# Gathering the rows of 64 of 512 prompt tokens in an expert-retrieval kernel, and multiplying the other 448 densely

## The reference, cut to what matters

```python
qry = (x @ w_query).reshape(tokens, 8, 2, 128)
s = einsum('thjd,jkd->thjk', qry, keys)
s_top, i_top = top_k(s, 16)
cand = s_top[:, :, 0, :, None] + s_top[:, :, 1, None, :]
cand_idx = i_top[:, :, 0, :, None] * 128 + i_top[:, :, 1, None, :]
best, pos = top_k(cand.reshape(tokens, 8, 256), 16)
idx = take_along_axis(cand_idx.reshape(tokens, 8, 256), pos)
gates = softmax(best)
act = gelu(einsum('thkd,td->thk', peer_u[idx], x))
out = einsum('thk,thkd->td', gates * act, peer_v[idx])
```

## Time and profile before

| | |
|---|---|
| median of three runs | 2342.01 us |
| the profiled execution, its own time | 2342.8 us |
| its span in the trace | 2341.0 us |
| mean granted clock of TensorE, share of full speed | 0.973 |
| busy share: TensorE, VectorE, ScalarE, GpSimd | 95%, 64%, 36%, 47% |
| DMA: bytes moved, mean rate | 392.79 MB, 168 GB/s |
| hide stage, units 0 to 127 | 852.8 to 1625.8 us |
| value products | 1625.8 to 2325 us |

### The profile page before, as it was taken

The page is one execution under the profiler, slowest core; times in us unless marked ns, Lnnn a source line. Parts: engine busy times, 40 slices in busy tenths (PEclk is TensorE's granted clock), DMA queues, the critical chain, the costliest instruction groups (busy, mean ns, idle before and its releaser), DMA issues.

```text
span 2341.0 us, 32763 instructions
## 1 busy us (share of the span) xinstructions
PE 2216.4 (95%) x12345; PEld 1887.8 (81%) x12345; DVE 1509.6 (64%) x3040; ACT 841.9 (36%) x1146; POOL 1099.7 (47%) x620
## 2 busy tenths in 40 slices
PE   5999999986998899999999999999999999999997
PEld 3998899864766888888887888888888888888886
DVE  4676569565554678887898786664655555555551
ACT  3433445563124233333243444453422222222221
POOL 1332336226443410877877656842644444444441
PEclk8999999996998999999999999999999999999998
DMA  8122122475656755777767897876754554554530
GB/s 281 56 91 72 44 75 90 123 198 175 187 185 233 258 164 144 153 143 146 144 132 157 222 273 197 177 186 202 276 202 181 213 191 170 215 197 169 207 144 36
DMA packets 320590, 392.79 MB, mean 168 GB/s; under 512 B 52305, under 2 KB 262629, under 8 KB 320194
## 3 DMA queue, kind: packets, MB, share of 16 engines
q1 hardware_dynamic: 216770, 302.86, 41.6%
q10 hardware_dynamic: 58768, 58.76, 7.5%
q0 software_dynamic: 44928, 29.51, 7.0%
HBM read 305.70 MB, written 81.39 MB: 165 GB/s over the span
## 4 chain that ended last, share of the span: by engine, by line
PE 45%; POOL 12%; issue 3%; DMA 2%; DVE 1%; ACT 0%; DVEq 0%; ACTq 0%; POOLq 0%
PE bank L2740 30%; PE bank L2169 13%; POOL gates_scattered_dram L2357 12%; PE bank L2686 2%; DMA gates_scattered_dram<-sel 2%; DMA work<-sample_rows_dram 1%; DVE harea L2159 0%; DVE work L2582 0%; PE bank L2692 0%; DVE harea L2145 0%; POOL work L2338 0%; PE bank L2760 0%; DVE work L2089 0%; DVE work L2105 0%; DVE work L2414 0%
## 5 line engine op out<-in xcount | busy, mean ns | idle before, releaser
L2169 PE MATMUL bank<-pH,harea 128*128 128x512 f32 x2048 | 647.7, 393 | 1.3 <-DVE harea L2159 1.3
L2357 POOL DMA_INDIRECT gates_scattered_dram<-sel x256 | 433.9, 1695 | 222.4 <-DVE sel L2420 94.6
L2169 PEld LDWEIGHTS bank<-pH,harea 128*128 128x128 f32 x2048 | 386.0, 188 | 82.2 <-DVE harea L2159 1.7
L2169 PE MATMUL bank<-pL,harea 128*128 128x512 f32 x1024 | 399.6, 390 | 0.0
L2740 PE MATMUL bank<-area,work 128*128 128x512 f32 x1536 | 350.8, 389 | 0.0
L2740 PEld LDWEIGHTS bank<-area,work 128*128 128x128 f32 x1536 | 288.4, 188 | 59.8
L2740 PE MATMUL bank<-harea,pH 128*128 128x512 f32 x1024 | 315.9, 390 | 0.0
L2346 POOL TENSOR_TENSOR work<-work,work 128x1024 fp32r<-128x1024 f32 x64 | 155.6, 2433 | 216.7 <-ACT work L2607 216.7
L2159 DVE TENSOR_TENSOR harea<-harea,harea 128x1024 fp32r<-128x1024 f32 x128 | 156.7, 1224 | 144.5 <-PE bank L2169 143.0
L2346 POOL TENSOR_TENSOR pL<-work,pH 128x1024 fp32r<-128x1024 f32 x64 | 155.2, 2426 | 194.0 <-ACT pH L2607 194.0
L824 POOL TENSOR_TENSOR wL_in<-wb_in,wH_in 128x1024 fp32r<-128x1024 f32 x52 | 129.4, 2489 | 240.7 <-ACT wH_in L777 240.7
(11 more groups left out here) (546 smaller groups left out, 3547.5 us busy)
## 6 DMA issues: line engine op xcount, KB each, us to landing
harea<-in_peer_u_dram SPq DMA_DIRECT2D x256, 256.0 KB, 10.0
work<-in_peer_v_dram SPq DMA_DIRECT2D x64, 1024.0 KB, 4.9
hidden_dram<-harea ACTq DMA_DIRECT2D x64, 512.0 KB, 2.7
wb_in<-in_w_in_dram SPq DMA_DIRECT2D x26, 1024.0 KB, 5.1
wstage<-in_w_ada_dram SPq DMA_DIRECT2D x32, 512.0 KB, 5.1
gates_scattered_dram<-work POOLq DMA_DIRECT2D x32, 512.0 KB, 5.6
gates_dram<-area ACTq DMA_DIRECT2D x8, 2048.0 KB, 12.5
area<-hidden_dram SPq DMA_DIRECT2D x16, 1024.0 KB
```

Source lines behind the costliest of these rows:

```text
L2169: mm = self.nc.tensor.matmul(self.pa[u % 2][:, :], w[:, k, :], x[:, k, :], start=(n == 0), stop=(n == 3 * KD - 1))
L2357: pool.indirect_dma_start(out=cells, out_offset=bass.IndirectOffsetOnAxis(ap=address_of[i][:, n:n + 1], axis=0), in_=gate_of[i][:, n:n + 1 ...
```

## The change

The constants become TG = 64, TD = 448, SC = 1. The last 64 prompt tokens, 448 to 511, no longer take part in the dense computation; they are treated as the sample tokens are.

- *Dense part.* hide and products have 448 columns, not 512; hidden activations, gates, weights and their buffers shrink alike.
- *Selection order.* TILES = (3, 0, 1, 2): tile 3, which holds the gathered tokens, is selected first, then tile 0, the only one that is scattered. The tokens 384 to 447 and the tiles 1 and 2 are placed in quads: 80 in all, 16 of them in every second unit from 26 to 56, the other 64 in units 74 to 121. Scatters are 128 and are spread over units 31 to 107 (scatters_by_unit), no longer ahead of the loop.
- *Buffers.* There is one staging buffer, so that each block's first eviction waits for the store of the block before it, and two PSUM banks for quads, not four. The freed memory holds the gathered rows: two of peer_u, four of peer_v.
- *Gathered tokens.* One token a unit, from unit 40: TensorE broadcasts token n's x to all partitions with two 512-column matmuls into two PSUM banks (cast, at the end of unit 40 + n, when dot n-1 is done); GpSimd gathers its 128 rows of peer_u (512 KB) up to two tokens ahead; VectorE takes the 128 dots at the end of loop 41 + n, reading x from PSUM. Every fourth unit ScalarE takes the Gelu of four tokens' dots, VectorE weighs them, GpSimd gathers four tokens' rows of peer_v (2 MB), and TensorE adds them up in eight float32 matmuls into a third bank (mix_gathered, 16 times, units 50 to 110). At the end the sums are turned and added to x.
- *Query phase.* 16 float32 matmuls turn the 64 tokens' x at n = 4; ScalarE rounds them into pH and pL at n = 6, VectorE subtracts at n = 7; SyncE's first load of peer_u waits for this turn and not for the sample tokens'.
- *Sample tokens.* Their mixes go to one PSUM bank in place of two, with the same number of matmuls.

The diff, cut to its core:

```diff
-SC = 2
+SC = 1
+TG = 64
+TD = T - TG
+TILES = (3, 0, 1, 2)
+SCATTERED = 1
...
-    for u in range(58, 74, 2):
+    for u in range(26, 58, 2):
         counts[u] = 1
-    total = (NC - SC) * L // 4
+    total = (TD - SC * L) // 4
...
+def scatters_by_unit():
+    counts = [0] * UNITS
+    for u in range(31, 40):
+        counts[u] = 2
+    for u in range(40, 80):
+        counts[u] = 2 if u % 4 != 3 else 0
+    for u in range(90, 107):
+        counts[u] = (1 if u < 99 else 2) if u % 4 != 3 else 0
+    counts[107] = SC * P - sum(counts)
...
+    STORED = [12, 13] + list(range(4, 12))
+    DOTS, GELUS, WEIGHS, GATHERS, MIXES = 40, 45, 48, 47, 50
...
-        stage = [carve(sc, 4096 * i, (P, NG, JG, TB)) for i in range(2)]
+        stage = carve(sc, 0, (P, NG, JG, TB))
+        vg = [carve(sc, 4096 + D * i, (P, D)) for i in range(4)]
+        ug = [carve(work, 9616 + D * i, (P, D)) for i in range(2)]
...
+            def gather_hidden(n):
...
+                if n >= 2:
+                    pool.wait_ge(G["dotted"], n - 1)
+                pool.indirect_dma_start(out=ug[n % 2], out_offset=None, in_=A["peer_u"][0], in_offset=index(n)).then_inc(G[f"ug_in{n % 2}"], 16)
+            def gather_values(i):
+                if i:
+                    pool.wait_ge(G["mixed"], i)
+                for n in range(4):
+                    pool.indirect_dma_start(out=vg[n], out_offset=None, in_=A["peer_v"][0], in_offset=index(4 * i + n)).then_inc(G["vg_in"], 16)
...
+                n = u - DOTS - 1
+                if 0 <= n < TG:
+                    dve.wait_ge(G[f"ug_in{n % 2}"], 16 * (n // 2 + 1))
+                    dve.wait_ge(G["cast"], n + 1)
+                    V.tensor_tensor_reduce(out=halves(ug[n % 2]), in0=halves(ug[n % 2]), in1=banks[:, 2:4, :], scale=1.0, scalar=0.0,
+                                           op0=ALU.mult, op1=ALU.add, accum_out=dot_g[:, n:n + 1]).then_inc(G["dotted"], 1)
...
-                b, blk = q // PER_BLOCK % 2, q // PER_BLOCK
-                if q % PER_BLOCK == 0 and blk >= 2:
-                    act.wait_ge(m[f"stored{b}"], 16 * (blk // 2))
+                blk, n = divmod(q, PER_BLOCK)
+                if n == 0 and blk:
+                    act.wait_ge(m["stored0"], 16 * blk)
...
+            def cast(n):
...
+                    pe.wait_ge(G["dotted"], n)
+                for half, x in enumerate((S.pH, S.pL)):
+                    mm = nc.tensor.matmul(bank[2 + half].rearrange("p (k n) -> p k n", k=KD), pick_g[:, n:n + 1].to_broadcast((P, P)), x[:, :, TD:T], start=True, stop=True)
+                mm.then_inc(G["cast"], 1)
+            def mix_gathered(n):
+                pe.wait_ge(G["weighed"], n + 1)
+                pe.wait_ge(G["vg_in"], 64 * (n + 1))
...
+                if DOTS <= u < DOTS + TG:
+                    cast(u - DOTS)
+                if u >= MIXES and (u - MIXES) % 4 == 0 and (u - MIXES) // 4 < TG // 4:
+                    mix_gathered((u - MIXES) // 4)
...
-                    mm = nc.tensor.matmul(bank[k], v[s][:, j, cols], w[s][:, j, :], start=(start and x == 0), stop=(stop and x == 2))
+                    mm = nc.tensor.matmul(bank[k][:, 0:TD], v[s][:, j, cols], w[s][:, j, :], start=(start and x == 0), stop=(stop and x == 2))
```

More of the change, by code:

```diff
@@ L1870, in _ @@
                     A_(halves(rows[:, :]), pt[0:B, :, :], ACT.Copy).then_inc(q["s_row"], 1)
+                if n == 6:
+                    act.wait_ge(q["x_turned"], 1)
+                    for half, x in enumerate((PH_, PL_)):
+                        rounded = A_(x[:, :, TD:T], pt[:, half, :].rearrange("p (k n) -> p k n", k=KD), ACT.Copy)
+                    rounded.then_inc(q["x_rounded"], 1)
             for n in range(CHUNKS - 2, CHUNKS):
@@ L1928, in _ @@
                     mm.then_inc(q["s_turned"], 1)
+                if n == 4:
+                    pe.wait_ge(q["s_row"], 1)
+                    for k in range(KD):
+                        for at in (0, TG):
+                            mm = nc.tensor.matmul(pt[at:at + TG, k // 4, k % 4 * P:k % 4 * P + P], hT[:, k, TD:T], S.ident[:, :], start=True, stop=True)
+                    mm.then_inc(q["x_turned"], 1)
                 if n >= 2:
@@ L2123, in __init__ @@
         self.u, self.ut, self.uv = S.hu, S.ut, S.uv
-        self.ge = [carve(S.harea, 6144 + 1024 * i, (P, 2, T)) for i in range(2)]
+        self.ge = [carve(S.harea, 6144 + 1024 * i, (P, 2, TD)) for i in range(2)]
         self.utH = carve(S.harea, 8192, (P, 3, KD, P), F32R)
@@ L2206, in quads_by_unit @@
     return [range(first[u], first[u + 1]) for u in range(UNITS)]
+def scatters_by_unit():
[7 more added lines that the diff above has]
+    counts[107] = SC * P - sum(counts)
+    first = [sum(counts[:u]) for u in range(UNITS + 1)]
+    assert first[UNITS] == SC * P and counts[107] > 0
+    return [range(first[u], first[u + 1]) for u in range(UNITS)]
 def expert_phase(nc, A, S, O, gates, scattered, hidden_dram, sample_rows):
@@ L2436, in select @@
                 elif s == 5:
-                    if i < SC:
+                    if i == SCATTERED:
                         dve.wait_ge(m["gates"], i + 1)
-                        K.gates(own, gate_of[i])
+                        K.gates(own, gate_of[0])
                     K.numbers(own, 0)
@@ L2520, in samples, with gathered @@
                     V.tensor_tensor(x_s, x_s, bcast(S.vec[:, V_GF:V_GF + KD], 2, B), ALU.mult).then_inc(e["s_y"], 1)
+            def gathered(u):
+                if u == 24:
+                    dve.wait_ge(m["res_s"], 1)
+                    V.tensor_tensor(pick_g[:, :], S.ident[:, 0:TG], S.ident[:, TG:P], ALU.add)
+                    V.memset(w_g[:, :, :, :], 0.0).then_inc(G["picked"], 1)
+                    own(V.tensor_scalar(act_g[:, :], S.sel[:, 0, TD:T], float(NKEY), None, ALU.mult))
+                    own(V.tensor_tensor(act_g[:, :], act_g[:, :], S.sel[:, 1, TD:T], ALU.add))
+                    V.tensor_copy(eu_g[:, :], act_g[:, :]).then_inc(G["numbered"], 1)
+                n = u - DOTS - 1
[4 more added lines that the diff above has]
+                                           op0=ALU.mult, op1=ALU.add, accum_out=dot_g[:, n:n + 1]).then_inc(G["dotted"], 1)
+                i = (u - WEIGHS) // 4
+                if (u - WEIGHS) % 4 == 0 and 0 <= i < TG // 4:
+                    dve.wait_ge(G["gelued"], i + 1)
+                    if i:
+                        dve.wait_ge(G["mixed"], i)
+                    pair = lambda t: t.rearrange("p (a b) -> p a b", a=2)
+                    V.tensor_tensor(w_g[:, :, :, 31], pair(act_g[:, 4 * i:4 * i + 4]), pair(S.sel[:, 2, TD + 4 * i:TD + 4 * i + 4]), ALU.mult).then_inc(G["weighed"], 1)
+                if u == MIXES + TG - 4 + 3:
+                    dve.wait_ge(G["turned"], 1)
+                    for k in range(KD):
+                        x = S.xT[:, k, TD:T].rearrange("p (i r) -> p i r", r=2)
+                        at = k % 4 * P + TG * (k // 4)
+                        last = V.scalar_tensor_tensor(out=x, in0=bank[5][:, at:at + TG].rearrange("p (r i) -> p i r", r=2), scalar=S.mod[:, 40 + k, 0:1],
+                                                      in1=x, op0=ALU.mult, op1=ALU.add)
+                    own(last)
             def weigh(s, j):
@@ L2541, in _ @@
                                        op0=ALU.mult, op1=ALU.add, accum_out=token[:, 0:1]))
-            own(V.tensor_scalar(token[:, 1:2], token[:, 0:1], float(P // TB * TB * JG), None, ALU.add))
             H.move_low(dve, 0)
@@ L2557, in _ @@
                 select_samples(u)
+                gathered(u)
                 samples(u)
@@ L2641, in _ @@
                     act.wait_ge(m["mixed_s"], B)
-                    nc.scalar.activation(halves(rows[0]), banks[:, 4:6, :], ACT.Copy).then_inc(m["mixed_rows"], 1)
+                    nc.scalar.activation(rows[0][:, 0:512], bank[4], ACT.Copy).then_inc(m["mixed_rows"], 1)
+                i = (u - GELUS) // 4
+                if (u - GELUS) % 4 == 0 and 0 <= i < TG // 4:
+                    act.wait_ge(G["dotted"], 4 * i + 4)
+                    nc.scalar.activation(act_g[:, 4 * i:4 * i + 4], dot_g[:, 4 * i:4 * i + 4], ACT.Gelu).then_inc(G["gelued"], 1)
+                if u == MIXES + TG - 4 + 1:
+                    act.wait_ge(G["mixed"], TG // 4)
+                    nc.scalar.activation(vg[0][:, 0:512], bank[5], ACT.Copy).then_inc(G["rows"], 1)
                 if u == 110:
@@ L2749, in group @@
                     for k in range(KD):
-                        if first and j == 0 and k == 4:
+                        if first and j == 0 and k == 2:
                             pe.wait_ge(e["s_row"], 1)
```

155 lines of the change are left out of this document (95 added, 60 removed).

## The result

The changed kernel takes 2390.74 us in the median of four runs (2389.05 to 2396.8), the kernel before 2342.68: a ratio of 1.0206 (95% interval 1.0186 to 1.0225). The forecast was 2349 us, with a range up to 2388. The profiled execution took 2396.8 us; its span is 2394.6, 53.6 longer than before's 2341.0. It is the slowest of the four, so that its rows show some 6 us more than the loss of 48 between the medians.

The account below looks back on a forecast made before the run. TensorE was taken to bound both expert stages. The terms -83 - 13 + 35 + 66 - 9 + 3 + 8 = +7 on the profiled 2342.8 us gave about 2349 us, with an 8-in-10 range of 2288 to 2388.

Parts of the forecast that it names:

- The clock, +8: TensorE, after store stalls and heavy loops: five gaps each lose 1.7 us to the 1.2 GHz level; +8 us (0 to 20).
- Products and the hide stage's matmuls, -83 each: Both expert stages on TensorE: 3072 matmuls each 27.1 ns shorter, -83 us a stage; new TensorE work nearly cancels the hide stage's.
- The lateness of the stores, +45: Units 74 to 103: gate-store landings beyond 12.5 us stall TensorE through the single staging buffer; 45 us of that stretch's +66.
- 9.1 / (1 - 0.488) = 17.8, so I go by that quotient: Stores of gates: shortest landing divided by the engines' share left beside GpSimd's queue, matching a landing of 17.6 us beside gathers.
- the share of 0.66: Units 80 to 91: GpSimd's queue share with sample gathers on top, giving 27 us landings and 14 us stall at two block ends.
- Units 41 to 73, +35: VectorE becomes the bound and casts wait for dots: 228 us against 193.2, +35 us (bounds +17 to +45).
- Units 104 to 127, -9: Last hide units: each 0.65 us shorter, less three more quads and two more mixes; -9 us.
- The query phase, +3: Query phase: 16 added fp32 matmuls on TensorE at 0.22 us each, nothing waiting for them; +3 us (0 to 5).
- Stores in time: Faster rival: gate-store landings stay under 12.5 us, so the 45 and the clock's 8 go; 2296 us, chance 0.26.
- Everything hidden: Faster rival: VectorE's overrun is absorbed too; 2252 us, chance 0.06.
- Late gathers: Slower rival: gathered rows arrive late, each of 64 tokens losing 0.6 us, 38 us more; 2387 us, chance 0.17.
- The pace that doesn't follow the columns: Slower rival: the weight load, not the column count, sets the matmul pace; 166 us more, 2515 us, chance 0.03.

Follow-up runs that it names:

- the run with many widths: Kernel before, with value products of 512 down to 256 columns across the eight output blocks: products in 602.6 us, 202.5 ns a matmul at 448 columns.
- the long runs: Changed kernel with the gates array in DRAM laid out partition by partition, so a block's store has 16 KB runs, not 512 B: 2354.67 us, 1.0048 of the kernel before.

## Why the prediction was wrong

The sum was +7 and the profiled execution's span grew by 53.6, so 47 us were missing (42 by the medians). Five terms came out worse than forecast, and one, the query phase, better.

**The clock, +8: wrong in size, about 15 us missing.** The step was "5 x 1.7": five gaps, each of which costs half of a 3.3-us stretch. In units 74 to 103 the mean clock of 0.87 means 2 x 0.13 x 292 = 76 us at 1.2 GHz. About half of it falls into the stalls themselves and costs nothing; but the three long stalls are followed by 9.0 + 7.9 + 8.0 us of it, two shorter ones by 6.8 and 6.0, 38 us in all. At 373 ns a matmul in place of 203 this loses 0.46 of its length, 17 us. The Trainium skill's page "TensorE: Matmul & The Clock Gate", section "HAM oscillation", puts the cost of a low clock at half its length; 0.46 agrees. In units 41 to 73 TensorE works at 1.2 GHz for 11.9 us, where before it was 3.4, and in units 0 to 40 for 9.0, where before it was 4.0: by the same 0.46 some 4 and 2 us more. The step failed in the length of the stretches. It was taken from one gap, and two of the long stretches follow gaps of 2.1 and 3.8 us, about as long as that one or shorter.

**Products and the hide stage's matmuls, -83 each: the pace, about 18 us missing.** The step was the straight line between 260 and 512 columns, 199.6 ns at 448; it was 202.7 in the products, as the run with many widths confirms (202.5). 3072 x 3.1 ns = 9.5 us in either stage.

**The lateness of the stores, +45: right in mechanism, 9 us missing.** All three steps were seen: the landing, ScalarE's wait for it, TensorE's wait two units later. The landings were forecast at 27, 27, 16.8 and (12.5 + 12) 24.5 us and came at 25.0, 36.8, 18.0 and 34.0; what they have over 12.5 sums to 64, not 45, and the waits came to 54, since somewhat more than 12.5 us is free. The step that failed is "9.1 / (1 - 0.488) = 17.8, so I go by that quotient". Over units 74 to 103 GpSimd's queue took 48.2% of the engines' time, nearly what it took in the earlier trace rows, and the four landings had a median of 29.5 us, where the quotient gives 17.6:

```profile
q0 software_dynamic: 15804, 45.27, 48.2%
...
gates_dram<-area ACTq DMA_DIRECT2D x4, 2048.0 KB, 29.5
```

While each of the four was under way, that queue's share was 43.9, 60.4, 36.3 and 54.2%, for which the quotient gives 16.2, 23.0, 14.3 and 19.9 us. That the forecast landings came nearer is luck: the share of 0.66 that the first two go by was too high. A share of time is not what a store of 512-byte packets gets: in the four landings 0.6 to 1.1 of the other two queues' packets were served for each of its own. The prediction had the packets' turn in a sentence beside the sum, with the upper bound of 65. That the stores are what the loss hangs on is shown by the long runs: 36 of the 48 us.

**Units 41 to 73, +35: right in mechanism.** The cast waits for the dot behind the selection step; moving the dot gave 13 us of the stretch back. Of the 10.8 us beyond the forecast, the pace makes 33 x 24 x 3.1 ns = 2.5 and the clock about 4; the dot itself took 1.18 + 0.08 us, less than the 1.35 of the sum. What makes the other 4 us is open.

**Units 104 to 127, -9:** -2.6, by the pace (2 us) and 5 us of idle time at three more block ends with landings of 13 us, which the sum did not count. **The query phase, +3,** was the term too large: -0.8, so the 16 matmuls cost nothing that can be told; the 0.22 us a matmul that it goes by does not stand in the earlier trace rows.

**The rivals.** Stores in time: excluded, by landings of 18 to 37 us. Everything hidden: excluded, by the 239 us of units 41 to 73. Late gathers gave nearly the right time, 2387, by a wrong way: in the changed kernel rows held up a dot by 2.9 us in all; they came next in line as soon as the stores were in time. The pace that doesn't follow the columns: excluded, but for 3 ns.

What stays open: why matmuls of 416 to 480 columns are 2 to 5 ns slower than the line; what decides how long the clock stays low behind a gap; by what order the DMA engines served the long runs; and what TensorE's 18 us of idle time in units 41 to 73 would need once the dots stand first; that it is light and heavy loops in lock-step was argued, not tried.

## What to carry to other kernels

Before costing a transfer that will run beside others, count packets as well as bytes: a store in 512-byte runs beside rows of 4 KB got a fifth of the engines' time, and laying out the array by partition (16 KB runs) cut its landing from 18 to 37 us to 10 to 11 with not a byte less; the short runs then fell to the loads that read the array back, where they cost nothing. A second buffer that shows no waits may be what hides exactly that. And where several waits stand in a row, each fix uncovers the next (stores, prompt rows, sample rows): only with the last of them did the kernel come out 1% faster than before.

## What the runs showed of the hardware that was not expected

A stall of 11 to 18 us left TensorE at the 1.2 GHz level for 8 to 9 us after its matmuls had started again. The length of the gap alone does not decide it: gaps of 2.1 and 3.8 us in the changed kernel were followed by 6.8 and 6.0 us at that level, the single 3.7-us gap of before by 3.3 us. And the pace of back-to-back matmuls is not quite straight in the columns: 189.5, 202.5, 211.4 and 215.5 ns at 416, 448, 464 and 480, against 186.1, 199.6, 206.4 and 213.2 on the line.
